# Joined block transposes, an own place for a third panel, one table load and a new order of the key norm in a hybrid encoder layer

## The reference, cut to what matters

```python
ada = silu(c) @ ada_w + ada_b
shift1, scale1, gate1, shift2, scale2, gate2 = split(ada, 6)
h = rms_norm(x, norm_mix_w) * (1 + scale1) + shift1
u = h @ w_in                                  # 8448 columns
# RWKV-7, on 1792 of these columns
u = u + (u_prev - u) * mu
r, k, v, w_lo, a_lo, g_lo = split(u)
decay = exp(-exp(-softplus(-(w0 + tanh(w_lo) @ w2)) - 0.5))
a = sigmoid(a0 + a_lo @ a2)
kk = heads(k * k_k)
kk = kk * rsqrt(max(sum(kk * kk), 1e-24))     # the key norm
k = k * (1 + (a - 1) * k_a)
# ... recurrence over time, then the bonus sum(r * k * r_k) * v
# attention: softmax(q k) twice per head, their difference times v, then rms_norm over the head
```

## Time and profile before

| | us |
|---|---|
| median of 3 runs | 1143.72 |
| lowest and highest run | 1143.09 and 1144.05 |
| the profiled execution | 1148.64 |
| its span | 1146.6 |

### The profile page before, as it was taken

How to read it: one execution, slowest core, us unless ns; L and a number is a source line. 1 busy time by engine, 2 the same in 40 slices (tenths; PEclk the granted TensorE clock), 3 DMA queues, 4 the chain that set the end, 5 groups by cost and what they waited for, 6 DMA issues and landing times.

```text
span 1146.6 us, 17320 instructions
## 1 busy us (share of the span) xinstructions
PE 1087.7 (95%) x7209; PEld 875.9 (76%) x7209; DVE 617.5 (54%) x853; ACT 472.4 (41%) x589; POOL 25.9 (2%) x45
## 2 busy tenths in 40 slices
PE   3999989999999999899998999999999999999997
PEld 2788756778888688778776777888888888878885
DVE  4478757345544257956845549754354343343336
ACT  6332551334232447666556665364212222132333
POOL 0100000100000000011000010000000000000000
PEclk9999988999999999999999999999999999999999
DMA  9858523320113532139421177512253423323201
GB/s 338 278 181 259 186 87 101 114 68 18 42 49 118 186 119 83 48 108 323 157 74 38 64 251 254 183 56 89 96 172 123 146 80 105 111 74 110 77 34 73
DMA packets 106773, 145.37 MB, mean 127 GB/s; under 512 B 3252, under 2 KB 86440, under 8 KB 106696
## 3 DMA queue, kind: packets, MB, share of 16 engines
q1 hardware_dynamic: 93544, 109.25, 29.2%
q0 software_dynamic: 5664, 21.38, 5.5%
q10 hardware_dynamic: 7488, 13.63, 3.2%
HBM read 128.53 MB, written 15.73 MB: 126 GB/s over the span
## 4 chain that ended last, share of the span: by engine, by line
PE 75%; DVE 13%; ACT 6%; issue 2%; DMA 2%; SPq 0%; ACTq 0%; POOL 0%; DVEq 0%
PE bank L2074 74%; DVE wlo L1378 2%; DVE Z L1378 2%; DMA cond<-in_ada_w 1%; DMA qk<-early_out 1%; DVE q_lev L1378 1%; DVE near L1818 1%; ACT whi L882 1%; ACT gate_row L897 1%; DVE SC L1378 0%; DVE mg L1378 0%; ACT L1290 0%; DVE Hb L1788 0%; ACT LX L1050 0%; DVE U L1378 0%
## 5 line engine op out<-in xcount | busy, mean ns | idle before, releaser
L2074 PE MATMUL bank<-hhi,whi 128*128 128x512 f32 (+1 forms) x816 | 327.8, 402 | 5.1 <-DVE hlo L1378 3.4
L2074 PE MATMUL bank<-hlo,whi 128*128 128x512 f32 (+1 forms) x816 | 319.4, 391 | 0.0
L2074 PE MATMUL bank<-hhi,wlo 128*128 128x512 f32 (+1 forms) x816 | 319.4, 391 | 0.0
L1378 DVE TENSOR_TENSOR wlo<-raw,whi 128x2048 fp32r<-128x2048 f32 (+1 forms) x79 | 168.3, 2130 | 253.5 <-ACT whi L882 252.6
L882 ACT ACTIVATE whi<-raw 128x2048 fp32r<-128x2048 f32 (+1 forms) x79 | 141.1, 1786 | 216.3 <-PE bank L2074 184.7
L2074 PEld LDWEIGHTS bank<-hhi,whi 128*128 128x128 f32 x816 | 156.3, 192 | 45.5 <-issue 6.0
L2074 PEld LDWEIGHTS bank<-hhi,wlo 128*128 128x128 f32 x816 | 156.2, 191 | 32.7
L2074 PEld LDWEIGHTS bank<-hlo,whi 128*128 128x128 f32 x816 | 156.2, 191 | 30.5 <-issue 0.5
L2074 PE MATMUL bank<-whi,d_hi 128*128 128x512 f32 x160 | 63.2, 395 | 1.2 <-DVE hid L1378 1.2
L2074 PE MATMUL bank<-whi,d_lo 128*128 128x512 f32 x160 | 63.1, 395 | 0.0
L2074 PE MATMUL bank<-wlo,d_hi 128*128 128x512 f32 x160 | 63.1, 395 | 0.0
(11 more groups left out here) (350 smaller groups left out, 1540.6 us busy)
## 6 DMA issues: line engine op xcount, KB each, us to landing
raw<-in_w_in SPq DMA_DIRECT2D x33, 1024.0 KB, 5.7
raw<-in_f_in SPq DMA_DIRECT2D x22, 1024.0 KB, 5.1
raw<-in_ada_w SPq DMA_DIRECT2D x16, 1024.0 KB, 5.4
early_out<-gate_row ACTq DMA_DIRECT2D x52, 256.0 KB, 2.1
raw<-in_f_out SPq DMA_DIRECT2D x11, 1024.0 KB, 5.1
cond<-in_ada_w SPq DMA_DIRECT2D x8, 1024.0 KB, 10.8
sg<-early_out POOLq DMA_DIRECT2D x4, 1536.0 KB, 11.1
raw<-in_w_out SPq DMA_DIRECT2D x4, 1024.0 KB, 5.1
```

The costliest lines, as they stand in the source:

```text
L1378: return v.tensor_tensor(out_, a, b, op)
L2074: return t.matmul(out_, lhsT, rhs, start=start, stop=stop, skip_group_check=True)
```

## The change

- Shift panels are treated as scale panels: `scale` and `scale_row` become `row`, for all eight first panels, with an own PSUM bank each; DVE's sums for them go, and `ada` has one part for each.
- x is scaled on DVE behind each reciprocal, not on ACT.
- PE's order in the start is new: two rows ahead of each quarter's transposes (the rows 4 and 5 each behind one `unit_part`), and each block pair of both panels behind its quarter.
- The third panel is split into `third_hi` and `third_lo`, which lie over `cond` 4 and 5, ahead of the last quarter on ACT and behind it on DVE. Later RWKV panels are split one turn earlier; the late sums move to the end of a turn.
- Sigmoids of w and a alternate on ACT.
- On DVE, kfac, the product K with it and the products r * k * r_k come before the clamp, and the split due at `rw kn` comes behind the reciprocal.
- ACT loads table set 6, which has a logarithm and an exponential, by hand ahead of HGRN2's norm.

The diff, cut to its core:

```diff
@@ -162 +163 @@
...
     total = len(panel_ends())
-    own = {total - spare: RING, total - spare + 2: RING + 2, total - 1: RING + 1}
+    own = {2: RING + 2, total - spare: RING, total - spare + 2: RING + 3, total - 1: RING + 1}
     shared = [m for m in range(total) if m not in own]
...
@@ -202 +203 @@
...
     for q in range(4):
-        b.add("scale", q)
+        b.add("row", 2 * q)
+        b.add("row", 2 * q + 1)
         if q == 0:
...
@@ -431 +433 @@
...
         cond = [at(f"cond{n}", 48 + 8 * n, [P, KC, 256]) for n in range(COND)]
+        third_hi = at("third_hi", 80, [P, 2048], F32R)
+        third_lo = at("third_lo", 88, [P, 2048], F32R)
         lev_f32 = at("lev_f32", 40, [P, 2 * RW_LEVELS + 1, 64])
...
@@ -669 +673 @@
...
         in_place = own_panel()
-        hi_slots = [whi[:, 0, :], whi[:, 1, :], spare_hi[:, :], last_hi, up_hi[:, :]]
-        lo_slots = [wlo[:, 0, :], wlo[:, 1, :], spare_lo[:, :], last_lo, raw_low[:, raw_place(weights[in_place])[0], :]]
+        hi_slots = [whi[:, 0, :], whi[:, 1, :], spare_hi[:, :], last_hi, third_hi[:, :], up_hi[:, :]]
+        lo_slots = [wlo[:, 0, :], wlo[:, 1, :], spare_lo[:, :], last_lo, third_lo[:, :], raw_low[:, raw_place(weights[in_place])[0], :]]
...
-            if f % 2:
-                eng.wait_ge(*full("scale", f // 2))
-            else:
-                eng.wait_ge(s_shift_sum, f // 2 + 1)
+            eng.wait_ge(*full("row", f))
...
@@ -868 +868 @@
...
+            def load_log_and_exp():
+
+                nc.scalar.add_instruction(mybir.InstLoadActFuncSet(
+                    name=nc.get_next_instruction_name(), act_func_set_id=LOG_AND_EXP, ins=[], outs=[]))
+
             def split_hi():
...
@@ -923 +928 @@
...
-            def scale_row(q):
-
-                act.wait_ge(*full("scale", q))
-                if q:
-                    act.wait_ge(*full("ada", 4 + q - 1))
-                do(ada_acc[:, 1, 0, :], bank_of("scale", q)[:, 0:256], ACT.Copy).then_inc(free_sem("scale", q), 1)
-                act.wait_ge(*freed("scale", q))
+            def row(f):
+
+                act.wait_ge(*full("row", f))
+                if f >= 2:
+                    act.wait_ge(*full("ada", ADA[f - 2]))
+                do(ada_acc[:, f % 2, 0, :], bank_of("row", f)[:, 0:256], ACT.Copy).then_inc(free_sem("row", f), 1)
+                act.wait_ge(*freed("row", f))
...
@@ -964 +969 @@
...
                 norm_root(0, tb, x_in, x_norm)
-            for tb in range(TB):
-                norm_scaled(0, tb, x_in, x_norm)
-            scale_row(0)
+            row(0)
+            row(1)
             split_hi()
...
             first_h(1)
-            scale_row(1)
+            row(2)
+            row(3)
             split_hi()
...
             first_h(3)
-            for q in range(2, 4):
-                scale_row(q)
-                first_h(2 * q)
-                first_h(2 * q + 1)
+            row(4)
+            row(5)
+            first_h(4)
+            first_h(5)
+            row(6)
+            row(7)
+            split_hi()
+            first_h(6)
+            first_h(7)
             for n in range(7):
-                if n:
+                if 0 < n < 6:
                     split_hi()
...
@@ -1003 +1013 @@
...
                 act.wait_ge(*freed("rw w", c))
-            act.wait_ge(s_rw_k_k, 4)
-            for c in range(4):
                 act.wait_ge(*full("rw a", c))
                 ps = bank_of("rw a", c)
+                if c == 0:
+                    act.wait_ge(s_rw_k_k, 4)
                 do(B[:, c, :], ps[:, :], ACT.Sigmoid, bias=vc[:, V_A0 + c:V_A0 + c + 1]).then_inc(free_sem("rw a", c), 1)
...
@@ -1227 +1237 @@
...
             act.wait_ge(s_roped, 1)
+            load_log_and_exp()
             for h in range(4):
...
@@ -1419 +1429 @@
...
-            def take_panel():
+            def take_low():
...
                 split_next[0] += 1
-                if m >= len(weights):
-                    return
                 i = weights[m]
...
@@ -1432 +1440 @@
...
                 dve.wait_ge(s_panel_taken, up(s_panel_taken))
+
+            def sums_behind(i):
+
                 while i + 1 < len(panels) and panels[i + 1][0] == "ada":
...
                     late_sum(i)
+
+            def take_panel():
+
+                m = split_next[0]
+                if m < len(weights):
+                    take_low()
+                    sums_behind(weights[m])
...
@@ -1506 +1524 @@
...
                 row_rstd(0, tb)
-            ada_sum(0, first_at[0])
+                ts(x_norm[:, tb, :], x_in[:, tb, :], col(RSTD + tb), ALU.mult).then_inc(s_x_normed, 1)
+                dve.wait_ge(s_x_normed, up(s_x_normed))
             conditioned(0)
...
             first_low(1)
-            ada_sum(1, first_at[2])
             conditioned(1)
...
             first_low(3)
-            ada_sum(2, first_at[4])
             conditioned(2)
-            ada_sum(3, first_at[6])
             first_low(4)
...
@@ -1526 +1542 @@
...
             first_low(7)
+            take_low()
...
             for n in range(7):
-                if n:
-                    take_panel()
                 for b in (2 * n, 2 * n + 1):
...
                     ada_out(ADA[8 + k])
+                if n < 5:
+                    sums_behind(weights[n + 2])
+                    take_low()
...
@@ -1559 +1577 @@
...
                 dve.wait_ge(s_rw_sums, up(s_rw_sums))
-            dve.wait_ge(*full("rw kk"))
-            ts(bonus[:, :], bank_of("rw kk")[0:8, :], 1e-24, ALU.max).then_inc(free_sem("rw kk"), 1)
-            dve.wait_ge(*freed("rw kk"))
-            early("rw kn")
             for c in range(4):
...
                 dve.wait_ge(s_dve_step, up(s_dve_step))
-            dve.wait_ge(s_rw_norm, 1)
-            v.reciprocal(bonus[:, :], bonus[:, :]).then_inc(s_rw_recip, 1)
-            dve.wait_ge(s_rw_recip, up(s_rw_recip))
             tt(K[:, :, :], K[:, :, :], kfac[:, :, :], ALU.mult).then_inc(s_dve_step, 1)
...
                 dve.wait_ge(s_rw_rkk, up(s_rw_rkk))
+            dve.wait_ge(*full("rw kk"))
+            ts(bonus[:, :], bank_of("rw kk")[0:8, :], 1e-24, ALU.max).then_inc(free_sem("rw kk"), 1)
+            dve.wait_ge(*freed("rw kk"))
+            dve.wait_ge(s_rw_norm, 1)
+            v.reciprocal(bonus[:, :], bonus[:, :]).then_inc(s_rw_recip, 1)
+            dve.wait_ge(s_rw_recip, up(s_rw_recip))
+            early("rw kn")
             for c in range(4):
...
@@ -2120 +2138 @@
...
-                if n < 4:
-                    pe.wait_ge(s_shift_sum, n + 1)
-                elif n < 8:
-                    pe.wait_ge(*freed("scale", n - 4))
+                if n < 8:
+                    pe.wait_ge(*freed("row", ADA.index(n)))
                 else:
...
-                parts = 1 if 4 <= n < 8 else 2
+                parts = 1 if n < 8 else 2
...
@@ -2143 +2159 @@
...
             def transposes(kcs):
-                pe.wait_ge(s_normed, TB)
+                pe.wait_ge(s_x_normed, TB)
                 for kc in kcs:
...
@@ -2187 +2203 @@
...
-            def scale(q):
-
-                src = loaded(pe, first_at[2 * q + 1]).rearrange("p (k n) -> p k n", k=KC)
-                ps = begin("scale", q)
+            def row(f):
+
+                src = loaded(pe, first_at[f]).rearrange("p (k n) -> p k n", k=KC)
+                ps = begin("row", f)
                 for k in range(KC):
...
                     last = mm(ps[rows, 0:256], ca_wide[:, k, :], src[:, k, :], k < 4, k >= KC - 4)
-                end(last, "scale", q)
+                end(last, "row", f)
...
@@ -2207 +2223 @@
...
-            scale(0)
+            row(0)
+            row(1)
             ada(0)
...
             transposes((0, 1))
-            scale(1)
+            units = [[begin("rw", 2 * n + m) for m in range(2)] for n in range(2)]
+            row(2)
+            row(3)
             transposes((2, 3))
...
             ada(5)
-            units = [[begin("rw", 2 * n + m) for m in range(2)] for n in range(2)]
             first = [next_panel()]
             unit_part(first[0], 0, units[0], (0, 1))
+            row(4)
             first.append(next_panel())
             unit_part(first[1], 1, units[1], (0, 1))
-            unit_part(first[0], 0, units[0], (2, 3))
-            scale(2)
+            row(5)
             transposes((4, 5))
...
             ada(6)
+            unit_part(first[0], 0, units[0], (2, 3))
             unit_part(first[1], 1, units[1], (2, 3))
-            scale(3)
+            row(6)
+            row(7)
             transposes((6, 7))
             ada(3)
+            ada(7)
             unit_part(first[0], 0, units[0], (4, 5))
-            ada(7)
+            unit_part(first[1], 1, units[1], (4, 5))
             unit_part(first[0], 0, units[0], (6, 7))
-            unit_part(first[1], 1, units[1], (4, 5))
             unit_part(first[1], 1, units[1], (6, 7))
...
```

More of the change, by code:

```diff
@@ L118 @@
 RING = 2
+LOG_AND_EXP = 6
 DOWN = 6
@@ L533, in build @@
```

(12 more changed lines are left out.)

## The result

The changed kernel takes **1124.18 us** (median of 4 executions, 1123.88 to 1125.07), beside 1143.88 for the kernel before (1143.09 to 1146.21): ratio 0.9826, 95% interval 0.9809 to 0.9843, 19.7 us less. The forecast was 1122.8, a gain of 20.9. In a later comparison the same file took 1123.57 (ratio 0.9810, 0.9793 to 0.9827).

A forecast was written before the change was run, and what follows sets the result against it. PE (TensorE), busy 95% of the span, was taken to bound the kernel. Start 4.5, sigmoids 2.4, the key norm's rest 7.8 and attention 6.2 sum to 20.9 us, taking 1143.7 to 1122.8; range 1113 to 1131.

The forecast's parts named there:

- start: Start to the third panel's first product: first panel product 1.3 us earlier, 3.2 saved after it, 4.5 in all.
- key norm: RWKV's key norm: alternating sigmoids save 2.4 us, DVE's new order and less low clock behind it 7.8.
- attention: Attention: one hand-placed load serves Ln and Exp, shortening PE's waits and removing a low stretch, 6.2 us.
- one low stretch 2.8: Start: panel products still lose 2.8 us to one stretch at the low clock, counted within 32.8 us after the change.
- 0 by itself: Third panel's earlier split in the start: no gain of its own, but it lets the start's 4.5 us be kept.
- the slack: Key norm: reciprocal ends at 159.5 and PE comes for it at 162.6, 3 us to spare.
- the other waits for the exponentials: Attention: PE's waits for exponentials other than the one at 606.28, 1.0 us in all, go.
- term (b): Key norm: DVE's new order removes PE's 2.88 us idle, and the eight bank products fall from 7.19 to 3.7.
- Rival 1: Attention: the hand-placed load changes nothing, as loads return before each Ln and Exp; 1129.0, chance 0.06.
- rival 2: Key norm: the wait only moves, as DVE's work ahead of the clamp eats the slack; 1130.6, chance 0.08.
- rivals 3 and 4: Start gains nothing, 1127.3, chance 0.14; or the clock never stays up there from 30.4 on, 1150, chance 0.03.
- rival 5: More than forecast: lora's low stretch gone, the start's first one shorter, the table-load drain rule; 1116, chance 0.12.

The follow-up runs named there:

- both: The changed kernel with ACT's squares, copies and split moved earlier at the key norm and panel products put between the 8-row products: 1122.87 us, ratio to before 0.9800.
- only_start: The kernel before with the start's part alone, including the third panel's own place: 1136.00 us, ratio 0.9927.
- spare_row: The kernel before with eight more PE products that nothing reads, ahead of the fourth conditioning row: 1144.79 us, ratio 0.9995.
- after_again: The changed kernel run again, unchanged: 1123.57 us, ratio to before 0.9810.
- only_norm: The kernel before with both key norm parts alone, alternating sigmoids and DVE's new order: 1137.35 us, ratio 0.9937.
- no_third: The changed kernel without the third panel's own place, with later panels split one turn later as before: 1129.38 us, ratio to before 0.9873.
- only_load: The kernel before with the attention's hand-placed table load alone: 1137.81 us, ratio 0.9951.
- only_order: The kernel before with DVE's new order at the key norm alone: 1139.11 us, ratio 0.9953.
- only_sig: The kernel before with the alternating sigmoids of w and a alone: 1142.27 us, ratio 0.9978.
- spread: The changed kernel with panel products put between the 8-row products at the key norm and ahead of the norm's variance: 1125.40 us, ratio to before 0.9828.

## Why the prediction was right, and which terms were off

The time, 1124.18, is 1.4 us above the forecast, and the mechanism of each part is the one forecast. The terms, with the parts run alone (or at the points of the traces):

| Term | forecast | alone | in the traces |
|---|---|---|---|
| start | 4.5 (0 to 6.5) | 8.4 (6.2 to 10.5) | 9.5 |
| key norm | 10.2 | 7.2 (4.9 to 9.5) | 9.9 |
| attention | 6.2 (2.5 to 8) | 5.6 (3.5 to 7.7) | 4.8 |
| sum | 20.9 | 21.2 | 24.0, with -0.2 elsewhere |

The whole gained 19.7 in the first comparison and 21.8 by the ratio of the second (0.019 x 1145.5). The sum came out right with one term too small and two somewhat large: alone, the start gave 3.9 more and the other two 3.6 less than forecast. That these cancel is luck.

**Start, too small.** The step that was mis-sized: "one low stretch 2.8" behind the first panel product, and the two `ada` at the low clock. Neither came in the trace of after. From 28.24 to 58.20 is 29.96 us, the forecast's own sum without that stretch (32.8 less 2.8 is 30.0). Ahead of it, row, transposes and `ada` took 4.5 us instead of 5.7. The remaining 0.9 is the earlier landing of the fourth panel, which differs between executions of one kernel. And the low stretch that I read as a fixed price is not one. In six profiled executions with the old start, full-rate work was first seen at 28.1 to 37.4 us; in seven with the new one at 23.7, 24.0, 24.4, 24.6, 27.4, 32.3 and 32.5. The third panel is begun at 64.3 to 67.8 us with the old start, at 57.2 to 60.7 with the new one and its own place for that panel, so the 9.5 of the two traces shown is near the most that a pair of them gives, and 8.4 alone fits them better. PE is busier ahead of it (13.6 us of 16 against 9.8). That the busier PE is the cause is argued from this, not shown: both and only_start have 13.3 and 13.2 busy us over 12 to 28 and still their full rate only at 32.3 and 32.5, and spare_row had an early clock with one row more, lost it in the wait for DVE, and gained nothing.

**Third panel's place.** Worth "0 by itself", but "what lets the 4.5 be kept", is borne out in kind: without it the gain shrinks by 5.2 us, through a wait of 2.53 us and the low stretch behind it. It kept more than 4.5 because the start gained more.

**Key norm, right in each step.** The 1.56 us became 0.50, 2.88 went, 7.19 became 3.70, the slack was 2.9 for 3. In the traces the sum closes: 1.1 + 1.7 (the low stretch at 143 to 147) + 2.9 + 5.1 (half rate and low clock behind, 6.8 less 1.7) less 0.8 for the new wait is 10.0, for 9.9 read at the points. Alone it gave 7.2 by the medians. A part of the difference is that the trace of before had every low stretch there, and not all executions do: from the third panel to the inverse five traces with the old key norm take 148.7, 148.7, 148.7, 147.3 and 145.7 us (less low clock in the last two), and the new one takes 138.6 to 138.8 in three (after, after_again, only_norm) and 141.9 in no_third, whose low stretch is twice as long. only_norm's own trace has 138.6, but it is one of its fastest executions (1134.92 for a median of 1137.35). Where the rest of the 2.7 us lies isn't shown. Missed was the gate row's wait, 0.8: the term (b) looked at DVE and the sum, not at ACT's own queue, where the copies stand behind the root, which waits for the clamp. The low stretch behind the 8-row products was forecast at 1.5 and cost 1.7.

**Attention, 0.6 to 1.4 too large,** though the interval alone (3.5 to 7.7) has room for the 6.2. 3.04 to 0.57 is 2.5, as forecast; the low stretch 1.7, forecast 1.8. Of the other waits for the exponentials, 1.0, 0.82 stayed, and the 0.9 at oa moved to the weight panels that DVE splits. That was the failed step: asking what is late next behind oa. 2.5 + 1.7 + 0.2 is 4.4, for 4.8 at the points. A table load begins right behind the function ahead of it, and the next function right behind its 1.28 us; timeline of before:

```profile
601.88 0.69 ACT L1290 ACTIVATE att<-bank,cst 128x512 f32<-128x512 f32 x1
602.59 1.28 ACT L1293 ACT_TABLE_LOAD   x1
603.88 0.63 ACT L1293 ACTIVATE att<-att 128x512 f32<-128x512 f32 x1
```

The Trainium skill (ScalarE: Activation LUTs, What ACT_TABLE_LOAD costs) adds a drain of 1.38 us to a switch. No such idle time is to be seen in these rows. The measured gain doesn't decide it, as its interval holds both sums, 6.2 and 6.7.

**Rivals.** Rival 1 (load ignored) fell by only_load, rival 2 (the wait moves) by only_order and only_sig, rivals 3 and 4 (start worth nothing, or worse) by only_start. Of rival 5 (more than forecast) two parts came, lora's low stretch gone and the first one shorter or absent, but 1116 was not reached. The Trainium skill (TensorE: Matmul & The Clock Gate, Part 4: PE-mode transpose) says that transposes don't count as busy in the same way; here the two rows, eight transposes and eight small products in one piece at 43.58 to 47.2 were followed by no fall: the clock column is 1.00 over 28 to 58 in after.

## What to carry to other kernels

Where PE waits for a sum on another engine and has idle time before a transfer lands, do the sum on PE, and look in the same change whether the next buffer will still be there when PE comes sooner: here the buffer was worth 5.2 us beside a start worth 8.4. A wait of 1.5 to 3 us on PE costs itself and in many traces 1.7 us of low clock behind it, and eight 8-row products in a row cost that too without any wait. Other products put between them held the clock up, but the changes and a bank that a busy ACT gives back late can cost as much as the clock does. Look where the time went, not at the clock alone: a low stretch in front of another wait was worth nothing. And take such prices from several executions: in two of the same code full rate was first seen at 37.4 and at 28.1 us.

## What was not expected of the hardware

- **The low clock behind the same idle time comes in some traces and not in others.** Its pieces cost 1.7 us each, or twice or four times that. Behind 2.8 us idle for h it came in seven of seven executions, behind 3.0 us for head 0 in six of seven (not in only_norm), behind 1.56 us in lora in four of six (not in only_order and only_start), behind 2.6 us for q_lev, the same in all fourteen, in five, and behind a second wait of 1.5 us for q_lev in none of nine. The two traces of before agree with each other at all of these places, and the two of after at those they still have, so whether it is chance from one execution to the next or follows from where in time the wait stands isn't shown.
- **Eight 8-row products in a row** at about 365 to 390 were followed by a low stretch in all twelve executions that have them so, without idle time in front; in fours with 512-column panel products between (spread, both) in neither of two.
- **The clock column does not show the slow beginning.** From 12 to 28 us it reads 1.00 in both kernels, while the same conditioning row takes 1.93 us there and 1.07 later.
- Scaling x on DVE took 0.75 us for 1024 columns, inside the bounds set (0.55 to 1.15).
